# Hybrid decoder trunk, RWKV steps: seven buffers instead of three for the split weight quarters, and seven quarters of each pair's weights split ahead of its step

## The reference, cut to what matters

```python
h = rmsnorm(x, attn_norm)
p = h @ a_w_in                      # r, k, v: 768 columns each; then decay, a, gate, q_mem
xs = p + (shift(p) - p) * mu
r, k, v, wd, ad, gd = split(xs)
...
def step(S, inp):                   # over the 512 tokens, state 64x64 per head
    sa = einsum('bhvk,bhk->bhv', S, -kk_t)
    S = S * w_t + outer(sa, kk_t * a_t) + outer(v_t, k_t)
    return S, einsum('bhvk,bhk->bhv', S, r_t)
```

## Time and profile before

| | |
|---|---|
| median of 3 runs | 1337.63 us (1337.31 to 1337.89) |
| the profiled execution | 1337.94 us, its span 1336.2 us |
| PE busy | 1289.4 us (96%) |
| DVE busy | 819.4 us (61%) |
| ACT busy | 582.3 us (44%) |
| POOL busy | 390.7 us (29%) |
| granted TensorE clock | full in all 40 slices |

### The profile page before, as it was taken

One profiled execution on the slowest core, in us unless ns is written; L12 is line 12 of the kernel. 1 busy time (PEld: TensorE's weight loads), 2 busy tenths in 40 slices (PEclk: granted clock), 3 DMA queues, 4 the chain that ended last, 5 costly groups with the idle time before them and its releaser, 6 DMA issues.

```text
span 1336.2 us, 25852 instructions
## 1 busy us (share of the span) xinstructions
PE 1289.4 (96%) x10448; PEld 1024.2 (77%) x10448; DVE 819.4 (61%) x1130; ACT 582.3 (44%) x904; POOL 390.7 (29%) x354
## 2 busy tenths in 40 slices
PE   6998989998999999999999999999999999999999
PEld 5866767776468888888888888776778888888887
DVE  4776778777566666246664447647576663366642
ACT  6574535553244444124444455457554441244421
POOL 3458779776620110001110145421111100011100
PEclk9999999999999999999999999999999999999999
DMA  8110111113222333223333243211133332233331
GB/s 319 48 33 20 54 38 53 37 36 115 80 74 84 96 99 124 90 79 95 94 118 103 75 142 95 63 48 33 32 95 94 94 130 78 89 98 94 118 110 39
DMA packets 30045, 114.22 MB, mean 85 GB/s; under 512 B 3456, under 2 KB 5248, under 8 KB 29184
## 3 DMA queue, kind: packets, MB, share of 16 engines
q1 hardware_dynamic: 29952, 112.89, 26.0%
HBM read 110.78 MB, written 2.10 MB: 84 GB/s over the span
## 4 chain that ended last, share of the span: by engine, by line
PE 75%; POOL 9%; DVE 6%; issue 3%; ACT 2%; POOLq 0%; DVEq 0%; ACTq 0%
PE bank L562 74%; POOL arena L2541 3%; POOL q_hi L2502 2%; POOL q_lo L2505 2%; POOL arena L2567 1%; PE bank L1232 1%; POOL arena L2537 1%; POOL arena L2535 1%; DVE head_stat L2276 1%; POOL w_lo L2639 1%; DVE sin_part L2266 0%; DVE cos_part L2293 0%; ACT w_hi L1312 0%; POOL roped L2631 0%; DVE in_lo L1911 0%
## 5 line engine op out<-in xcount | busy, mean ns | idle before, releaser
L1312 ACT ACTIVATE w_hi<-ring 128x1024 fp32r<-128x1024 f32 (+1 forms) x144 | 162.3, 1127 | 262.5 <-PE bank L562 262.5
L562 PE MATMUL bank<-in_hi,w_hi 128*128 128x512 f32 x704 | 274.9, 390 | 0.9 <-DVE in_lo L1911 0.9
L562 PE MATMUL bank<-in_hi,w_lo 128*128 128x512 f32 x704 | 273.9, 389 | 0.0
L562 PE MATMUL bank<-in_lo,w_hi 128*128 128x512 f32 x704 | 273.9, 389 | 0.0
L2614 POOL TENSOR_TENSOR z_raw<-silu,conv 128x512 f32<-128x512 f32 x40 | 51.5, 1288 | 538.1 <-DVE conv L2217 503.7
L1886 DVE TENSOR_TENSOR w_lo<-ring,w_hi 128x1024 fp32r<-128x1024 f32 (+1 forms) x124 | 165.2, 1332 | 64.9 <-ACT w_hi L1312 64.5
L562 PEld LDWEIGHTS bank<-in_hi,w_hi 128*128 128x128 f32 x704 | 132.2, 188 | 29.5 <-DVE in_lo L1911 1.4
L562 PEld LDWEIGHTS bank<-in_lo,w_hi 128*128 128x128 f32 x704 | 132.2, 188 | 27.9 <-issue 0.5
L562 PEld LDWEIGHTS bank<-in_hi,w_lo 128*128 128x128 f32 x704 | 132.2, 188 | 27.3
L562 PEld LDWEIGHTS bank<-arena 64*64 64x64 f32 (+2 forms) x4064 | 109.9, 136 | 54.5 <-issue 35.3
L562 PE MATMUL bank<-arena 64*64 64x64 f32 (+4 forms) x4064 | 133.4, 239 | 12.1 <-ACT arena L1470 4.0
(11 more groups left out here) (263 smaller groups left out, 2178.5 us busy)
## 6 DMA issues: line engine op xcount, KB each, us to landing
ring<-w_ring SPq DMA_DIRECT2D x119, 512.0 KB, 3.5
ring<-w_ring SPq DMA_DIRECT2D x32, 704.0 KB, 4.1
ring<-w_pairs SPq DMA_DIRECT2D x18, 512.0 KB, 3.6
arena<-w_mem SPq DMA_DIRECT2D x2, 2048.0 KB, 19.8
arena<-w_ring SPq DMA_DIRECT2D x4, 512.0 KB, 4.9
x<-xT SPq DMA_DIRECT2D x1, 2048.0 KB, 8.0
outT<-x SPq DMA_DIRECT2D x8, 256.0 KB, 2.0
mask<-masks SPq DMA_DIRECT2D x1, 1536.0 KB, 6.8
```

Source lines behind the costliest of these rows:

```text
L562: return nc.tensor.matmul(out, lhsT, rhs, start=first, stop=last, skip_group_check=True)
L1312: return nc.scalar.activation(out, in_, ACT.Copy)
```

## The change

The number of buffers for split quarters of the pairs goes from three to seven. The first three stay `q_hi` and `q_lo`; four more pairs of 128x256 lie in ring memory that nothing uses then: five blocks of slot 3 and the 384 columns behind the tile in each of slots 0 to 2. The quarters of the first four weight tiles (before the pairs) keep three buffers. With seven buffers, GpSimd splits quarters 0 to 6 of a pair ahead of `fS` and `XT` of its step (before: 0 to 2); quarters 3, 4, 5 and 6 are gone from between the masks. Quarter 7 now follows `mask(2)` and quarter 8 follows `mask(3)`, so ahead of `bb`; quarters 9 to 11 follow `mask(4)`. For pair 0 seven quarters instead of three stand ahead of the copy L2517. The number of instructions that compute is the same, and their shapes are too. A quarter now waits for the one seven before it.

```diff
-QSLOTS = 3
+OSLOTS = 3
+QSLOTS = 7
...
+        with ExitStack() as in_ring:
+            ends = []
+            for i in range(SLOTS - 1):
+                tensor(in_ring, f"below_end_{i}", [P, TILEW])
+                ends.append(tensor(in_ring, f"end_{i}", [P, SLOTW - TILEW], F32R))
+            last_slot = tensor(in_ring, "last_slot", [P, SLOTW], F32R)
         ring = sb("ring", [P, SLOTS, SLOTW])
...
+        spare = [last_slot[:, i * QW:(i + 1) * QW] for i in range(5)] + [end[:, 0:QW] for end in ends]
+
+        def quarter_parts(n):
+            w = n % OSLOTS if n < Q0 else (n - Q0) % QSLOTS
+            if w < OSLOTS:
+                return q_hi[:, w, :], q_lo[:, w, :]
+            return spare[2 * (w - OSLOTS):2 * (w - OSLOTS) + 2]
...
             def split_quarter(j, g):
...
-                if j is None:
-                    pass
-                elif g == QSLOTS - 1 and j == 0:
+                o = n - Q0 - QSLOTS
+                if n == Q0:
                     pool.wait_ge(used, N_OUTA)
-                elif g == QSLOTS - 1:
-                    pool.wait_ge(sem("krv_mm"), 3 * j)
-                elif (g - QSLOTS) % 4 == 3:
-                    pool.wait_ge(sem("krv_mm"), 3 * j + (g - QSLOTS) // 4 + 1)
-                else:
-                    o = g - QSLOTS
-                    pool.wait_ge(sem("q_used"), 9 * j + (3 * N_OUTA + 3 * (o // 4) + o % 4 + 1))
+                elif o >= 0 and o % 4 == 3:
+                    pool.wait_ge(sem("krv_mm"), o // 4 + 1)
+                elif o >= 0:
+                    pool.wait_ge(sem("q_used"), 3 * (N_OUTA + o // 4) + o % 4 + 1)
...
                 mask(0)
-                quarter(3)
                 mask(1)
-                quarter(4)
                 if back:
...
                     G.tensor_copy(Rp, AR[:, 1, :, :]).then_inc(sem("r_in"), 1)
-                quarter(5)
                 mask(2)
-                quarter(6)
+                quarter(7)
                 mask(3)
-                quarter(7)
+                quarter(8)
                 if front:
...
                 mask(4)
-                for g in range(8, 12):
+                for g in range(9, 12):
                     quarter(g)
```

More of the change, by code:

```diff
@@ L144, in sem, with tensor @@
             return made[name]
+        def tensor(group, name, shape, dt=F32):
+            return group.enter_context(nc.sbuf_tensor(name, shape, dt))
         y = sb("y", [P, KD, T])
+        with ExitStack() as in_ring:
[4 more added lines that the diff above has]
+            last_slot = tensor(in_ring, "last_slot", [P, SLOTW], F32R)
         ring = sb("ring", [P, SLOTS, SLOTW])
@@ L158, in trunk @@
         head_stat = sb("head_stat", [P, 2, RES, 8])
-        def tensor(group, name, shape, dt=F32):
-            return group.enter_context(nc.sbuf_tensor(name, shape, dt))
         with ExitStack() as rwkv_layer:
@@ L166, in trunk @@
             h_hi = tensor(rwkv_layer, "h_hi", [P, KD, T], F32R)
-            q_hi = tensor(rwkv_layer, "q_hi", [P, QSLOTS, QW], F32R)
-            q_lo = tensor(rwkv_layer, "q_lo", [P, QSLOTS, QW], F32R)
+            q_hi = tensor(rwkv_layer, "q_hi", [P, OSLOTS, QW], F32R)
+            q_lo = tensor(rwkv_layer, "q_lo", [P, OSLOTS, QW], F32R)
             arena = tensor(rwkv_layer, "arena", [P, ARENA])
@@ L588, in quarter @@
                 n = g if j is None else Q0 + 12 * j + g
-                w = (g if j is None else Q0 + g) % QSLOTS
+                high, low = quarter_parts(n)
                 pe.wait_ge(sem("q_split"), n + 1)
@@ L594, in quarter @@
                         pe.wait_ge(sem("h_ready"), k + 1)
-                    mm(out, q_hi[:, w, ks], h_hi[:, k, :], first and b == 0, False)
-                    mm(out, q_hi[:, w, ks], h_lo[:, k, :], False, False)
-                    q = mm(out, q_lo[:, w, ks], h_hi[:, k, :], False, last and b == 1)
+                    mm(out, high[:, ks], h_hi[:, k, :], first and b == 0, False)
+                    mm(out, high[:, ks], h_lo[:, k, :], False, False)
+                    q = mm(out, low[:, ks], h_hi[:, k, :], False, last and b == 1)
                 return q
@@ L1325, in weights_high @@
                     act.wait_ge(landed[g // 4], 16)
-                o = g - QSLOTS
+                o = g - OSLOTS
                 if o >= 0 and o % 4 == 3:
@@ L1330, in weights_high @@
                     act.wait_ge(sem("q_used"), 3 * (o // 4) + o % 4 + 1)
-                copy(q_hi[:, g % QSLOTS, :], ring[:, g // 4, (g % 4) * QW:(g % 4 + 1) * QW]).then_inc(sem("q_high"), 1)
+                copy(quarter_parts(g)[0], ring[:, g // 4, (g % 4) * QW:(g % 4 + 1) * QW]).then_inc(sem("q_high"), 1)
             def query_out(i):
@@ L2484, in split_quarter @@
                 t = g // 4
-                w = (g if j is None else Q0 + g) % QSLOTS
+                n = g if j is None else Q0 + 12 * j + g
+                high, low = quarter_parts(n)
                 if g % 4 == 0 and j is not None:
                     pool.wait_ge(sem(f"wp_in{t}"), 16 * (j + 1))
-                if j is None:
-                    pass
-                elif g == QSLOTS - 1 and j == 0:
+                o = n - Q0 - QSLOTS
+                if n == Q0:
                     pool.wait_ge(used, N_OUTA)
-                elif g == QSLOTS - 1:
-                    pool.wait_ge(sem("krv_mm"), 3 * j)
-                elif (g - QSLOTS) % 4 == 3:
-                    pool.wait_ge(sem("krv_mm"), 3 * j + (g - QSLOTS) // 4 + 1)
-                else:
-                    o = g - QSLOTS
-                    pool.wait_ge(sem("q_used"), 9 * j + (3 * N_OUTA + 3 * (o // 4) + o % 4 + 1))
+                elif o >= 0 and o % 4 == 3:
+                    pool.wait_ge(sem("krv_mm"), o // 4 + 1)
+                elif o >= 0:
+                    pool.wait_ge(sem("q_used"), 3 * (N_OUTA + o // 4) + o % 4 + 1)
                 src = ring[:, t, (g % 4) * QW:(g % 4 + 1) * QW]
-                n = g if j is None else Q0 + 12 * j + g
                 if j is not None:
-                    G.tensor_tensor(q_hi[:, w, :], src, ones[:, 0:1].to_broadcast([P, QW]), ALU.mult)\
-                        .then_inc(sem("q_high"), 1)
+                    G.tensor_tensor(high, src, ones[:, 0:1].to_broadcast([P, QW]), ALU.mult).then_inc(sem("q_high"), 1)
                 pool.wait_ge(sem("q_high"), n + 1)
-                G.tensor_tensor(q_lo[:, w, :], src, q_hi[:, w, :].bitcast(F32), ALU.subtract).then_inc(sem("q_split"), 1)
+                G.tensor_tensor(low, src, high.bitcast(F32), ALU.subtract).then_inc(sem("q_split"), 1)
             for g in range(Q0):
```

## The result

The changed kernel takes 1330.59 us (median of 6 runs, 1329.13 to 1334.2), the kernel before 1337.8 (6 runs, 1337.31 to 1339.03). The ratio is 0.994, with the interval 0.9925 to 0.9954. That is 8.0 us faster by the ratio, 7.2 by the medians. A second measurement on another chip gave 0.9936 (0.9921 to 0.9951). The direction was right, the size was not: 5.3 us were forecast. Two executions of the kernel before on other chips, of 1828.48 and 7260.93 us, are slow ones and enter no ratio.

What follows compares the result with a forecast made beforehand. TensorE's waits for GpSimd's split quarters were taken as the bound, with VectorE to watch. Steps 2 to 5 gave 4.2 us, step 1 0.8, step 0 0.3: 5.3 us, so 1332.3 us, range 1330.2 to 1336.6.

Steps and rivals of the forecast that it cites:

- What bounds the kernel: RWKV steps: TensorE's waits for split quarters count, 6.4 us for `q_lo`, not GpSimd's 9% of the chain.
- Part 1: TensorE's waits for quarters 7 and 8 and `wg_lo` go: credit 6.4 us, and 0.18 x 4 for `wg_lo`.
- Part 2: Whether VectorE keeps pace: steps 2 to 5 gain 1.05 us each, 4.2 in all; step 1 gains 0.8.
- first stretch: VectorE up to `wg_lo`: 4.55 us instead of 5.2, gate product about 0.6 us earlier out of 0.73.
- second stretch: VectorE from L2098 to the last `inverse_add`, 9.0 us: net 0.3 to 0.7 us earlier, out of 0.56.
- discount for VectorE: Steps 2 to 5: VectorE's collisions with GpSimd let only 0.6 and 0.45 us of TensorE's waits be gained.
- upper bound: Steps 2 to 5: at most 1.3 us each, if all three of TensorE's waits go.
- first rival: VectorE's turns add up as today, TensorE's waits become waits for VectorE: gain 1.5 us, 1336.1; chance 0.25.
- Part 3: Step 0 and the moved work: seven quarters done before `XT`, tight in step 1; 0.3 us of 0.89 kept.
- `XT` comes late: Rival: quarters cost 2.1 us instead of 1.4, step 1's seven end 4 us later: 1337.5; chance 0.05.
- VectorE takes it back: The first rival: waits for `q_lo` become waits for `wg_lo` and `inverse_add`; gain 1.5 us, 1336.1; chance 0.25.
- The collision with `tri_d` decides: Rival, bonus to last `inverse_add`: two operations wait for whole instructions, 0.3 x 5 steps slower, 1339.1; chance 0.08.

Runs made afterwards that it cites:

- Kernel 1: The changed kernel's seven buffers, but three quarters split ahead and GpSimd's old order; ratio 0.9987 to the kernel before.
- kernel 10: The changed kernel with quarter 8 put back behind `bb` and `mask(4)`; ratio 0.9945 to the kernel before.
- kernel 7: The changed kernel with four buffers and four quarters ahead, quarter 8 still ahead of `bb`; ratio 0.9958 to the kernel before.
- kernel 3: The kernel before with four buffers and four quarters ahead, quarter 8 still behind `bb` and `mask(4)`; ratio 0.9985 to the kernel before.
- kernel 2: The kernel before, three buffers and three ahead, with only quarter 8 moved ahead of `bb` and `mask(4)`; ratio 0.9968 to it.
- Kernel 4: The changed kernel, but only four quarters split ahead for pair 1, seven for the others; ratio 0.9926 to the kernel before.
- kernel 6: The kernel before with VectorE's `wg_lo` moved ahead of the bonus and gate; ratio 1.0029 to the kernel before.
- 8: Kernel 4 with `wg_lo` moved ahead of the bonus and gate in all steps; ratio 0.9936 to the kernel before.
- 9: Kernel 4 with `wg_lo` moved ahead of the bonus and gate in step 6 alone; ratio 0.9928 to the kernel before.
- 5: Kernel 3 with VectorE's `wg_lo` moved ahead of L2094 and L2096; ratio 0.9964 to the kernel before.

## Why the prediction came out as it did

**What bounds the kernel: right.** The sum was made from TensorE's waits and not from GpSimd's 9% of the chain, and it was of the right order. Kernel 1 shows that in steps 1 to 5 GpSimd's queue and not the buffers held the quarters up.

**Part 1: right.** The waits for quarters 7 and 8 and for `wg_lo` are gone in steps 1 to 5. With seven ahead the place of quarter 8 makes no difference there (kernel 10); with four ahead it is worth 2.0 us (kernel 7 against 3); and alone, with three ahead, it only moves a wait (kernel 2). So it is the number ahead that does it.

**Part 2 is the step that failed, in size.** It took 0.6 of the first stretch's 0.73 us and 0.45 of the second's 0.56, 1.05 per step. Measured are 0.87 and 0.64, 1.51 in step 3. Two terms were wrong, by 0.24 and 0.20 us a step.

First, the discount for VectorE (1.29 down to 1.05) was not due: TensorE has no wait for VectorE at all. The forecast of VectorE's first stretch was close, 4.55 us where 4.37 is measured. L2094 was to wait 1.2 us for `mask(4)`; it waits 0.71 for `y` and then for what is left of `mask(4)`, 0.43, together 1.14. But `wg_lo` ends only 0.06 us before TensorE wants it, so 0.18 us more would have delayed the gate product by about as much (an estimate from these two ends). In the second stretch L2121 takes 1.53 us as forecast, L2128 to L2134 1.10 to 1.21, and the stretch is 0.64 shorter, at the upper end of the 0.3 to 0.7 forecast. So the discount failed by a margin, and not because VectorE was out of play.

Second, the upper bound itself was too low. It was the sum of the idle times printed ahead of three matmuls, 1.3 us. By starts the same three cost 0.63, 0.24 and 0.62, 1.49. The product ahead of quarter 7 is drawn 0.62 us long, but without a wait quarter 7 starts 0.55 behind it, so a gap is printed shorter than it delays. Starts measured from a common event would have given it: `kkss` to quarter 7 took 1.18 us before and takes 0.55 now.

The working behind Part 2 is confirmed in the other respect: VectorE can decide. With four ahead the quarters' waits are just as absent, and it takes back 0.87 to 1.27 us of each step (kernel 3); that is the first rival, and it holds for that kernel. What separates it from the changed one is where GpSimd stands when `kkr` comes. In the changed kernel it has been waiting 0.56 us for it, so `bb` falls on VectorE's transposes and L2091. In kernel 3 it comes to `bb` late, after quarter 7, and both long instructions fall on L2094 and L2096. The Trainium skill has this in "SBUF — State Buffer", section "SBUF: two separate sides": whichever starts first keeps the shared port pair for its whole instruction. The trace agrees to 0.01 us: in kernel 3 L2094 starts at 213.07, `bb` ends at 214.24, and 1.17 of waiting and 0.55 of its own make 1.72, against 1.73. The 0.55 is an estimate from the changed kernel, where L2094 takes 0.98 with 0.43 of `mask(4)` left.

**Part 3: the mechanism right, the split off, the sum right by luck.** Steps 0 and 1 were to give 0.3 and 0.8, 1.1 together; A gained 1.32. Up to step 1's first quarter TensorE gains 1.44 us. Most of it is quarter 8: from `kkss` to the memory product behind that quarter it took 4.69 us before and takes 3.52 now, 1.17 less, where a wait of 0.89 was printed; and `kkss` itself comes 0.20 earlier, which the forecast had no term for. Behind it the changed kernel gives nothing, it loses 0.12. Step 1's `XT` was forecast 0.6 us later than due; it is 1.8 us behind the gram part, with no idle time on GpSimd ahead of it. Kernel 4 shows that this costs 1.2 us; with `XT` on time step 1 gives 1.05. The rival "`XT` comes late" was thus real in step 1, but its place is step 1 alone: in steps 2 to 5 GpSimd still waits 4 us ahead of `fS`, as forecast.

**Sum.** Forecast 4.2 for steps 2 to 5 and 1.1 for the rest; measured 6.0 and 1.3. The error is the 1.8 us of Part 2, in four steps 1.0 for the discount and 0.8 for the bound. By the prediction's own bounds the most is 5.2 + 0.95 + 1.4 = 7.55 and the low end 1330.1, not 1330.2; the 1329.6 lies below either.

**The rivals.** "VectorE takes it back" fell for the changed kernel and holds for kernel 3. "The collision with `tri_d` decides" fell: L2118 takes 0.74 us (0.68 before) instead of waiting for a whole instruction, only L2121 meets `tri_d` for 1.53, and the stretch is 8.35 us, not 10.2. Among the signs named, `fS` still waits for ScalarE, GpSimd waits 1.46 us for the k tile, and step 1's `XT` has no wait for VectorE; `pq_product` was put at 29.9 and is at 29.43.

**What stays open.** In kernels 2 and 6 most of what A and B don't hold goes with the executions' clock, but not all that is measured: kernel 3's A and B give 2.7 us, its eight executions at a mean clock of 1.0 only 1.3. Open too is which of kernels 4, 8 and 9 is fastest. Kernel 4 is ahead of the changed kernel by 0.0014 in ratio with overlapping intervals, but by 1.2 us in A, which repeats to 0.03 us in the two pairs of profiles taken of one kernel.

## What to carry to other kernels

Where two engines take turns on a port, what an earlier start is worth depends on which instruction of the other engine the long ones fall on: write down both engines' order at the stretch, and give the one with long instructions enough lead that it waits for its input before them. Price a wait of TensorE by the starts of its matmuls from a common event, with and without the wait, not by the idle time printed ahead of them. Compare kernels by executions of the same granted clock, and look for stretches of lower clock in a profile before explaining a difference in it. And count the work moved ahead for each iteration on its own: the first one had 3.72 us of room for four more quarters, the others 7.5.

## What the runs showed of the hardware

Some of TensorE's waits on "issue", in which the profile shows nothing it waits for, stand in the same place in every profile (about 0.4 to 0.5 us behind `pq_product`, 0.92 to 0.95 in step 6); the longest and those between belong to the execution and not to the kernel. The second profile of the kernel before took 1342.54 us against 1337.94 of the first. A and B are the same in them to 0.03 us. Between 320 and 372 us the second has five such waits, 0.31, 0.79, 3.69, 0.95 and 1.21 us, the first has four, 0.58, 0.52, 0.92 and 0.58. The longest of the second:

```profile
340.89 0.57 PE L562 MATMUL bank<-arena 64*64 64x64 f32 x23 [3.69 <-issue]
```

Behind it the clock fell: with TensorE busy again from 340.9 us on, the granted clock was 0.64 from 340 to 345 us and 0.68 from 345 to 350, with 0.50 (1.2 GHz) in each whole microsecond from 342 to 348. In the first profile it was 1.00 throughout this time. So the 4.4 us between the two are idle time and the slower matmuls behind it. The profiles of kernels 1, 2, 5 and 9 have stretches of lower clock too, of some 3 to 7 us each, and TensorE stood idle shortly before every one of them. An idle time does not always bring a fall: the changed kernel waits 1.93 us on "issue" at 331.21 and keeps its clock at 1.00. Of the executions whose clock is on record, 28 of 68 of the kernel before and 9 of 12 of the changed one have a mean of 1.0; in every group those at 0.997 or below are 2.0 to 7.8 us longer on average than those at 1.0.

The changed kernel's two profiles differ in their waits on "issue" as well (0.16 and 0.29 us in steps 3 and 5 of one, 0.17 and 0.56 in steps 2 and 3 of the other). So a single profile says little on a microsecond unless it is read stretch by stretch. What causes these waits, and which of them the clock falls behind, no run here shows.

Moving one operation within VectorE's queue, with no change in work, cost 2.0 us in steps 2 to 5 (kernel 6; 3.9 by the ratio), through the turns that the operations behind it then took.
